# A hybrid SSD / RWKV-7 / mLSTM diffusion step on one core: the three output norms moved

## What is computed

```python
def _group_norm(y, g, n_groups, center, eps=1e-5):
    yf = y.reshape(y.shape[:-1] + (n_groups, y.shape[-1] // n_groups))
    if center:
        yf = yf - jnp.mean(yf, axis=-1, keepdims=True)
    yf = yf * lax.rsqrt(jnp.mean(yf * yf, axis=-1, keepdims=True) + eps)
    return yf.reshape(y.shape) * g
# SSD, 512 features, 2 groups of 256
y = (y_f + y_b + d_skip[:, None] * xs).reshape(b, t, D_SSD) * jax.nn.silu(z)
y_ssd = _group_norm(y, norm_g, SSD_GROUPS, center=False)
# RWKV-7, 256 features, 4 heads of 64 (o_f, o_b hold the bonus of r, k, r_k and v)
y_rwkv = _group_norm((o_f + o_b).reshape(b, t, D_RWKV), norm_g, RWKV_HEADS, center=True) * gate
# mLSTM, 256 features, 4 heads of 64
y_ml = _group_norm((h_f + h_b).reshape(b, t, D_MLSTM), norm_g, MLSTM_HEADS, center=True) * jax.nn.sigmoid(o)
y = jnp.concatenate([y_ssd, y_rwkv, y_ml], axis=-1) @ p['w_out']
```

## Time and profile before

| | us |
|---|---|
| median of 3 runs (lowest, highest) | 2300.25 (2297.17, 2303.04) |
| the profiled execution | 2307.51 |
| its span, mean granted clock 0.962 | 2305.8 |
| TensorE busy, products | 2129.9 (92%) |
| TensorE busy, weight loads | 1974.0 (86%) |
| VectorE busy | 836.0 (36%) |
| ScalarE busy | 774.3 (34%) |
| GpSimd busy | 735.9 (32%) |
| moved by DMA | 166.67 MB, 72 GB/s on the mean |

### The profile page before, as it was taken

One profiled execution on the slowest core, in us unless ns is written; L12 is line 12 of the kernel. 1 busy time (PEld: TensorE's weight loads), 2 busy tenths in 40 slices (PEclk: granted clock), 3 DMA queues, 4 the chain that ended last, 5 costly groups with the idle time before them and its releaser, 6 DMA issues.

```text
span 2305.8 us, 46139 instructions
## 1 busy us (share of the span) xinstructions
PE 2129.9 (92%) x20590; PEld 1974.0 (86%) x20590; DVE 836.0 (36%) x1385; ACT 774.3 (34%) x1368; POOL 735.9 (32%) x539
## 2 busy tenths in 40 slices
PE   4999999888789999999979989988888899999999
PEld 4999766778589999999979987667867899999998
DVE  4755265554641111011148443555455311110112
ACT  3535553323333222121144364433332422222212
POOL 4333161324123333333313322522242233333331
PEclk7999998999899999999989999899998899999999
DMA  7454201000012222234335431010001122222222
GB/s 250 147 156 128 63 8 37 6 2 3 19 55 65 80 76 74 74 110 142 104 87 174 148 114 30 1 38 5 3 2 46 50 79 74 74 74 74 73 76 71
DMA packets 260497, 166.67 MB, mean 72 GB/s; under 512 B 29938, under 2 KB 234228, under 8 KB 260300
## 3 DMA queue, kind: packets, MB, share of 16 engines
q1 hardware_dynamic: 259846, 163.59, 23.9%
q10 hardware_dynamic: 454, 0.14, 0.0%
HBM read 159.59 MB, written 4.12 MB: 71 GB/s over the span
## 4 chain that ended last, share of the span: by engine, by line
PE 84%; DVE 7%; ACT 5%; issue 2%; POOL 1%; DMA 0%; another core or an unknown queue 0%; SPq 0%; DVEq 0%; ACTq 0%
PE PS L928 21%; PE PS L929 20%; PE PS L930 20%; PE PS L1317 5%; PE PS L892 2%; PE PS L1462 1%; PE PS L1146 1%; PE PS L1383 1%; PE PS L1335 1%; PE PS L1183 1%; PE PS L989 1%; DVE U L2330 1%; PE PS L1197 1%; POOL ring_r L810 1%; PE PS L1150 1%
## 5 line engine op out<-in xcount | busy, mean ns | idle before, releaser
L928 PE MATMUL PS<-rwp_r,whi_r 128*128 128x320 f32 x2880 | 904.5, 314 | 40.4 <-POOL ring_r L810 16.5
L930 PE MATMUL PS<-rwp_r,ring_r 128*128 128x320 f32 x2880 | 896.6, 311 | 0.0
L810 POOL TENSOR_TENSOR ring_r<-ring,whi_r 128x1024 fp32r<-128x1024 f32 (+1 forms) x204 | 498.5, 2445 | 1139.7 <-ACT whi_r L1647 1139.7
L929 PE MATMUL PS<-arena_r,whi_r 128*128 128x320 f32 x2240 | 697.4, 311 | 0.0
L928 PEld LDWEIGHTS PS<-rwp_r,whi_r 128*128 128x128 f32 x2880 | 547.0, 190 | 56.0 <-issue 28.6
L930 PEld LDWEIGHTS PS<-rwp_r,ring_r 128*128 128x128 f32 x2880 | 546.9, 190 | 0.0
L929 PEld LDWEIGHTS PS<-arena_r,whi_r 128*128 128x128 f32 x2240 | 425.4, 190 | 0.0
L1647 ACT ACTIVATE whi_r<-ring 128x1024 fp32r<-128x1024 f32 (+1 forms) x204 | 211.4, 1039 | 542.1 <-PE PS L930 542.0
L929 PE MATMUL PS<-U_r,whi_r 128*128 128x320 f32 x960 | 298.2, 311 | 0.0
L2542 DVE TENSOR_TENSOR U<-arena,PS 128x640 f32<-128x640 f32 x44 | 36.2, 822 | 549.7 <-PE PS L930 549.7
L929 PEld LDWEIGHTS PS<-U_r,whi_r 128*128 128x128 f32 x960 | 181.8, 189 | 0.0
(11 more groups left out here) (383 smaller groups left out, 2667.7 us busy)
## 6 DMA issues: line engine op xcount, KB each, us to landing
ring<-in_ffn_w SPq DMA_DIRECT2D x120, 512.0 KB, 3.8
rwp<-in_ada_w SPq DMA_DIRECT2D x64, 512.0 KB, 4.8
ring<-in_w_in SPq DMA_DIRECT2D x50, 512.0 KB, 4.4
U<-in_ada_w SPq DMA_DIRECT2D x16, 512.0 KB, 9.7
ring<-in_w_out SPq DMA_DIRECT2D x16, 512.0 KB, 4.6
arena<-in_ada_w SPq DMA_DIRECT2D x16, 512.0 KB, 4.7
ring<-in_ffn_w SPq DMA_DIRECT2D x16, 384.0 KB, 3.3
out<-arena SPq DMA_DIRECT2D x5, 512.0 KB, 2.6
```

What stands on the lines that cost most here:

```text
L810: g.tensor_tensor(rings_r[:, slot_of[n], 0:size(n), :], slot(n)[:, 0:size(n), :], whis[:, q_ % 2, 0:size(n), :].bitcast(F32), ALU.subtract ...
L928: mm(out, w[0][:, k, :], hi[:, cols], start=start, stop=False)
L929: mm(out, w[0][:, k, :], lo[:, cols], start=False, stop=False)
L930: return mm(out, w[1][:, k, :], hi[:, cols], start=False, stop=stop)
```

## The change

SSD and mLSTM take their norms in two parts. In the scan, the sum of squares: for SSD, GpSimd multiplies each chunk by its gate (`gate(c)`), ScalarE squares it (`y_squares`), TensorE sums over features with a column of ones, so that a chunk's sums come with tokens on partitions (`y_sums`), VectorE copies them (`y_variance`). For mLSTM, `normalise` adds the two directions, centres, squares and sums with tokens on partitions (five VectorE instructions more), and `mlstm_back` is two transpositions in place of four products with the identity. The 30 columns `YN` of sums (2 groups and 4 heads, 5 chunks) get their square root on ScalarE at the end of RWKV's step 0 and their reciprocal on VectorE in step 1. `norm_rows`, in SyncE's queue ahead of w_out's block 2, writes them to DRAM with tokens as the last axis and reads them back broadcast over partitions, into `RBS` (SSD, in `whi`) and `ring_rows` (mLSTM, in the ring slot of block 2), and then waits until both are used. VectorE scales SSD's four tiles at the end of step 2, scales and gates mLSTM's two at the end of step 3. Their splits: `y_high` of three tiles at the end of step 3 and of three in step 4, `y_low` of three in step 4 and of three behind it.

The norm block keeps RWKV's own norm (centring, variance, one square root and one reciprocal of 64 partitions, scaling and gate), placed between w_out's rows: rows of tiles 0 to 2, centring, row 3, variance, rows 4 and 5, then the spread, then RWKV's two tiles. `YSEQ` is this order of the K tiles. A dummy square root stands ahead of it on ScalarE. The idle products are fewer: `warm` 6 to 2 and 8 to 4.

```diff
...
+yn_d = [nc.dram_tensor("yn%d" % l, (6, NC * P), F32, kind="Internal").ap() for l in range(DEPTH)]
...
+YSQ = [ar(9472 + 512 * i, 512) for i in range(2)]
+YS, YMEAN = ar(10496, 256), ar(4904, 4)
+RBS = whif[:, 0:2 * T].rearrange("p (g t) -> p g t", g=2)
...
+YSEQ = [0, 1, 2, 3, 6, 7, 4, 5]
+def ring_rows(lay):
+  at_ = KT * P * slot_of[SPLIT[lay * Q_LAYER + Q_WOUT + 2]]
+  return ring[:, at_:at_ + 2 * T].rearrange("p (f t) -> p f t", f=2)
...
+  def norm_rows():
+    sp.wait_ge(s["yn_rec"], at["yn_rec"] + 1)
+    load(yn_d[lay].rearrange("r (c t) -> t (r c)", c=NC), YN[:, :], s["yn_out"])
+    sp.wait_ge(s["yn_out"], at["yn_out"] + 16)
+    load(RBS, yn_d[lay][0:2].unsqueeze(0).broadcast_to((P, 2, T)), s["yn_in"])
+    for q in range(2):
+      load(ring_rows(lay)[64 * q:64 * q + 64],
+        yn_d[lay][2 + q:6:2].unsqueeze(0).broadcast_to((64, 2, T)), s["yn_in"])
+    sp.wait_ge(s["y_done"], at["y_done"] + 6)
   def rwkv_out():
...
+    if blk == (lay, "w_out", 2):
+      norm_rows()
...
   def gates():
-    pool.wait_ge(s["yt_read"], at["yt_read"] + NC)
-    pool.wait_ge(s["ys_read"], at["ys_read"] + NC)
-    g.tensor_tensor(U[:, XS:XS + 4, :], U[:, XS:XS + 4, :], U[:, Z:Z + 4, :], ALU.mult).then_inc(
-      s["gated"], 1)
-    pool.wait_ge(s["gated"], at["gated"] + 1)
-    pool.wait_ge(s["rw_ready"], at["rw_ready"] + 1)
...
+  def gate(c):
+    pool.wait_ge(s["ys_read"], at["ys_read"] + c + 1)
+    g.tensor_tensor(U[:, XS:XS + 4, ck(c)], U[:, XS:XS + 4, ck(c)], U[:, Z:Z + 4, ck(c)],
+            ALU.mult).then_inc(s["gated"], 1)
   def skip(c):
...
+      gate(c - 2)
+    for c in range(NC - 2, NC):
+      gate(c)
   def chunk_keys(k):
...
+  def y_sums(c):
+    pe.wait_ge(s["ysq_ready"], at["ysq_ready"] + c + 1)
+    for q in range(4):
+      n = 384 + 2 * c + q // 2
+      ins = mm(PS[:, 0, n:n + 1], YSQ[c % 2][:, q * P:(q + 1) * P], ones[:, 0:1],
+          start=q % 2 == 0, stop=q % 2 == 1)
+    ins.then_inc(s["ysq_mm"], 1)
   def y_mlstm(c):
...
-      for d in range(2):
-        ins = mm(PS[:, 6, f * P:(f + 1) * P], YM[:, d, f * P:(f + 1) * P], ident[:, :],
-            start=d == 0, stop=d == 1)
+      ins = tr(PS[:, 6, f * P:(f + 1) * P], YM[:, 0, f * P:(f + 1) * P], ident[:, :])
...
+      if c > 1:
+        y_sums(c - 2)
...
-  warm(6, 2)
+  y_sums(NC - 3)
+  warm(2, 2)
...
+  for c in range(NC - 2, NC):
+    y_sums(c)
   def cpos(k, d):
...
+  pe.wait_ge(s["ysq_read"], at["ysq_read"] + NC)
...
-        warm(8, 7)
+        warm(4, 7)
...
-  for n, t_ in enumerate((Z, Z + 1, MV, MV + 1)):
-    g_job(2 * n, [(BO[:, :], U[:, t_, :])]).then_inc(s["g_mm"], 1)
-  pe.wait_ge(s["g_read"], at["g_read"] + 4)
...
-    g_job(2 * ((2 + i) % 4), [(SPREAD[rows, :], gtmp[rows, 3, :])]).then_inc(s["g_mm"], 1)
   def residual_mm(b, w, k, hi, lo, start, stop):
...
-  pe.wait_ge(s["y_done"], at["y_done"] + 6)
+  def out_rows(seq):
+    for n in seq:
+      k = YSEQ[n]
+      pe.wait_ge(s["y_lo"], at["y_lo"] + n + 1)
+      for m in range(2):
+        ins = residual_mm(4 + 2 * m, w01[m], k, rp_r[:, k, :], U_r[:, YTILES[k], :], n == 0,
+                 n == KT - 1)
+        if n == KT - 1:
+          ins.then_inc(s["wo_mm"], 1)
+  for f in range(2):
+    g_job(2 * f, [(BO[:, :], U[:, Z + f, :])]).then_inc(s["g_mm"], 1)
...
-  for k, t_ in enumerate(YTILES):
-    pe.wait_ge(s["y_lo"], at["y_lo"] + k + 1)
-    for m in range(2):
-      ins = residual_mm(4 + 2 * m, w01[m], k, rp_r[:, k, :], U_r[:, t_, :], k == 0, k == KT - 1)
-      if k == KT - 1:
-        ins.then_inc(s["wo_mm"], 1)
+  out_rows(range(3))
+  pe.wait_ge(s["g_src"], at["g_src"] + 1)
+  for f in range(2):
+    g_job(2 * f, [(BO[:, :], U[:, BT_ + f, :])]).then_inc(s["g_mm"], 1)
+  out_rows(range(3, 4))
+  for f in range(2):
+    pe.wait_ge(s["g_read"], at["g_read"] + 4)
+    pe.wait_ge(s["g_sq"], at["g_sq"] + f + 1)
+    ins = g_job(0, [(BO[:, 48:80], gtmp[:, f, :])], slice(32 * f, 32 * f + 32))
+  ins.then_inc(s["g_mm"], 1)
+  out_rows(range(4, 6))
+  pe.wait_ge(s["g_rec"], at["g_rec"] + 1)
+  for f in range(2):
+    rows = slice(32 * f, 32 * f + 32)
+    g_job(2 * f, [(SPREAD[rows, :], gtmp[rows, 3, :])]).then_inc(s["g_mm"], 1)
+  out_rows(range(6, 8))
...
+  def y_squares(c):
+    act.wait_ge(s["gated"], at["gated"] + c + 1)
+    if c == 0:
+      act.wait_ge(s["stored"], at["stored"] + 7 * 16)
+    if c > 1:
+      act.wait_ge(s["ysq_mm"], at["ysq_mm"] + c - 1)
+    A(YSQ[c % 2].rearrange("p (f t) -> p f t", f=4), U[:, XS:XS + 4, ck(c)], ACT.Square).then_inc(
+      s["ysq_ready"], 1)
...
+      if i == 4 and c > 1:
+        y_squares(c - 2)
...
+  for c in range(NC - 2, NC):
+    y_squares(c)
+  def y_high(seq):
+    act.wait_ge(s["rw_feat"], at["rw_feat"] + 2 * NC)
+    act.wait_ge(s["rs_dve"], at["rs_dve"] + 2 * NC)
+    for n in seq:
+      act.wait_ge(s["y_done"], at["y_done"] + n + 1)
+      A(rp_r[:, YSEQ[n], :], U[:, YTILES[YSEQ[n]], :], ACT.Copy).then_inc(s["y_hi"], 1)
   def decays(k):
...
+    else:
+      y_high(range(3, 6))
...
+      act.wait_ge(s["ysq_read"], at["ysq_read"] + NC)
+      A(YN[:, 0:2 * NC], YN[:, 0:2 * NC], ACT.Sqrt, bias=eps[:, 2:3], scale=1.0 / 256)
+      A(YN[:, 2 * NC:], YN[:, 2 * NC:], ACT.Sqrt, bias=eps[:, 2:3], scale=1.0 / 64).then_inc(
+        s["yn_std"], 1)
+    if k == NC - 2:
+      y_high(range(3))
...
-  act.wait_ge(s["gated"], at["gated"] + 1)
-  act.wait_ge(s["yr_read"], at["yr_read"] + 2 * NC)
-  for q in range(4):
...
-    A(SQUARES[n], U[:, t_, :], ACT.Square).then_inc(s["g_sq"], 1)
+  A(NSD[:, :], NRC[:, :], ACT.Sqrt)
+  for f in range(2):
+    act.wait_ge(s["g_read"], at["g_read"] + 3 + f)
+    A(gtmp[:, f, :], U[:, BT_ + f, :], ACT.Square).then_inc(s["g_sq"], 1)
...
-  A(gtmp[0:64, 2, :].rearrange("p (a t) -> p a t", a=2), PS[0:64, 6:8, 0:HALF], ACT.Sqrt,
-   bias=eps[0:64, 2:3], scale=1.0 / 256).then_inc(s["g_std"], 1)
-  act.wait_ge(s["g_mm"], at["g_mm"] + 8)
-  A(gtmp[:, 3, :].rearrange("p (a t) -> p a t", a=2), PS[:, 4:6, 0:HALF], ACT.Sqrt,
-   bias=eps[:, 2:3], scale=1.0 / 64).then_inc(s["g_std"], 1)
-  for k, t_ in enumerate(YTILES):
-    act.wait_ge(s["y_done"], at["y_done"] + k + 1)
-    A(rp_r[:, k, :], U[:, t_, :], ACT.Copy).then_inc(s["y_hi"], 1)
+  A(gtmp[0:64, 3, :].rearrange("p (a t) -> p a t", a=2), PS[0:64, 0:2, 0:HALF], ACT.Sqrt,
+   bias=eps[0:64, 2:3], scale=1.0 / 64).then_inc(s["g_std"], 1)
+  y_high(range(6, 8))
...
-              (P, 2, 4, 64)), ALU.mult).then_inc(s["ym_ready"], 1)
+              (P, 2, 4, 64)), ALU.mult).then_inc(s["dve_step"], 1)
+    dve.wait_ge(s["dve_step"], step())
+    v.tensor_tensor(YS, YM[:, 0], YM[:, 1], ALU.add).then_inc(s["dve_step"], 1)
+    dve.wait_ge(s["dve_step"], step())
+    v.tensor_reduce(YMEAN, heads(YS, 4), AX.X, ALU.add).then_inc(s["dve_step"], 1)
+    dve.wait_ge(s["dve_step"], step())
+    v.scalar_tensor_tensor(out=heads(YM[:, 0], 4), in0=wide(YMEAN, 64), scalar=-1.0 / 64,
+               in1=heads(YS, 4), op0=ALU.mult, op1=ALU.add).then_inc(s["ym_ready"], 1)
+    dve.wait_ge(s["ym_ready"], at["ym_ready"] + c + 1)
+    v.tensor_tensor(YM[:, 1], YM[:, 0], YM[:, 0], ALU.mult).then_inc(s["dve_step"], 1)
+    dve.wait_ge(s["dve_step"], step())
+    v.tensor_reduce(YN[:, 2 * NC + c::NC], heads(YM[:, 1], 4), AX.X, ALU.add).then_inc(
+      s["dve_step"], 1)
+    dve.wait_ge(s["dve_step"], step())
+  def y_variance(c):
+    dve.wait_ge(s["ysq_mm"], at["ysq_mm"] + c + 1)
+    v.tensor_copy(YN[:, c:2 * NC:NC], PS[:, 0, 384 + 2 * c:386 + 2 * c]).then_inc(s["ysq_read"], 1)
   def prep_scan(k):
...
+    if c > 2:
+      y_variance(c - 3)
...
+  dve.wait_ge(s["ysq_mm"], at["ysq_mm"] + NC)
+  for c in range(NC - 3, NC):
+    y_variance(c)
   def chunk_start(k):
...
+  def y_scale(t_, nm, f, rows):
+    return v.scalar_tensor_tensor(out=U[:, t_, :], in0=U[:, t_, :], scalar=col(lay, nm, f),
+                   in1=rows, op0=ALU.mult, op1=ALU.mult)
+  def y_low(n):
+    k = YSEQ[n]
+    dve.wait_ge(s["y_hi"], at["y_hi"] + n + 1)
+    v.tensor_tensor(U_r[:, YTILES[k], :], U[:, YTILES[k], :], rp_r[:, k, :].bitcast(F32),
+            ALU.subtract).then_inc(s["y_lo"], 1)
...
+    else:
+      for n in range(3):
+        y_low(n)
+    if k == 1:
+      dve.wait_ge(s["yn_std"], at["yn_std"] + 1)
+      v.reciprocal(YN[:, :], YN[:, :]).then_inc(s["yn_rec"], 1)
...
+    if k == 2:
+      dve.wait_ge(s["yn_in"], at["yn_in"] + 16 * 3)
+      for f in range(4):
+        y_scale(XS + f, "ssd_norm_g", f, RBS[:, f // 2, :]).then_inc(s["y_done"], 1)
+    if k == 3:
+      for f in range(2):
+        ins = y_scale(MV + f, "mlstm_norm_g", f, ring_rows(lay)[:, f])
+      ins.then_inc(s["dve_step"], 1)
+      dve.wait_ge(s["dve_step"], step())
+      for f in range(2):
+        v.tensor_tensor(U[:, MV + f, :], U[:, MV + f, :], U[:, MO + f, :],
+                ALU.mult).then_inc(s["y_done"], 1)
+  for n in range(3, 6):
+    y_low(n)
   def pair(ap):
...
-  for n in range(2):
-    centre(MV + n, 4 + 2 * n, 3 + n)
...
-    centre(BT_ + n, 2 * n, 6 + n)
```

(16 more changed lines are left out.)

64 lines of the change are left out of this document (7 added, 57 removed).

## The result

The changed kernel takes 2354.73 us (median of 4 runs, 2342.99 to 2363.03), the kernel before 2298.71 us beside it: 2.5% slower, ratio 1.0247, 95% interval 1.0205 to 1.0289. The forecast was 2297, with a range up to 2315. The profiled execution of the changed kernel took 2357.4 us, the one of before 2307.51.

What follows compares the result with a forecast made beforehand. TensorE's chain (84%) bounds the kernel, its long hole per layer being the norm block. Per layer -19.7 (tail) + 7.4 (scan) + 9.1 (RWKV) + 1.8 (clock) = -1.4; twice -2.8 from 2300.25 gives 2297 us, range 2280 to 2315.

Steps and rivals of the forecast that it cites:

- SP's queue: SyncE's queue in RWKV: row write and read back estimated at 20 us against 58 available, so cost 0.
- the rows come late: Rival, end of step 2: 4-byte pieces take 100 us, VectorE and the recurrence stand; +50 per layer, 2400; chance 0.02.
- The scan: Scan: mLSTM's five VectorE passes delay the next decay products; together +7.4 us per layer (4.5 to 9.5).
- My steps: Scan terms: chunks 0 to 1 +2.3, 1 to 2 +1.5, 2 to 3 0, 3 to 4 +1.5, end +1.05 and +1.1.
- RWKV's steps: RWKV: step 1 +0.35, step 2's end +2.0, step 3's end +2.05, step 4 +4.7; together +9.1 us per layer.
- The +4.7 for the low halves of step 4: RWKV step 4: three y_low on VectorE held by GpSimd's port use, making the two adds behind late; +4.7 us.
- the sign that I had named: Step 4: y_low longer than 0.82 us beside GpSimd's scalings; running at 0.82 would mean the forecast is wrong, faster.
- the faster rival: Rival, step 4: y_low is not held by GpSimd's scalings; -7.0 us per layer, 2286; chance 0.34.
- the lower end of my bound: RWKV step 4: three y_low running bare, with the queue behind them, cost at least +0.4 us.
- The tail: Norm block behind RWKV's last add: 29.0 us in place of 48.8, at the full clock; 19.7 us less per layer.
- The clock rival: Rival: new TensorE holes bring 1.2 GHz in scan (4.4 us), two step ends and tail; +9.5 per layer, 2319; chance 0.22.
- 1.8 us for one hole: RWKV step 4: a TensorE hole of 4.6 us lowers the clock; 1.8 us counted per layer, other holes left uncounted.

Runs made afterwards that it cites:

- e1_rows: The changed kernel with the sums written to DRAM as 128 pieces of 120 bytes in place of 3840 of 4 bytes; 2327.48 us, ratio 1.0103.
- b2_write: The kernel before plus one DMA per layer, 30 idle columns written in 3840 pieces of 4 bytes in RWKV's step 1; 2326.63 us, ratio 1.0117.
- e2_no_mlstm: The changed kernel without mLSTM's five VectorE passes per chunk in the scan, directions added by four products as before; 2323.41 us, ratio 1.0102.
- e3_no_ssd: The changed kernel without SSD's squares, sums and their copies in the scan, a constant standing in; 2345.22 us, ratio 1.0169.
- e4_fill: The changed kernel with eight more idle products of 512 columns per chunk (1 to 4) on TensorE; 2330.95 us, ratio 1.0127.
- e9_all: The changed kernel with sums written in 512-byte pieces, scan passes, scalings and low halves moved, tail reordered, idle products added; 2281.21 us, ratio 0.9922.
- e10_nofill: As e9_all without its idle products (none in the scan, 2 and 4 behind it); 2267.41 us, ratio 0.9853 to the kernel before.

## Why the prediction was wrong

**SP's queue: the step that failed.** I costed the row write at 0, "unless a piece costs over four times that". The sentence asks only who waits for the rows, and in that it was right: the read back was in the rows' place by 495.5 and was needed at 542.6. It doesn't ask what the write does to an engine that doesn't wait for it. The price of a piece was not too low: 11.7 ns against the 34 that I took. But the queue went on only 17 us after the issue, and TensorE's semaphore came up to 6.8 us late meanwhile. The write cost 14.2 and 8.8 us (e1_rows, b2_write), nearly half of the loss. My rival "the rows come late" had the right culprit with the wrong victim, and only 0.02.

The Trainium skill, Runtime: NRT & Kernel Launch, section Instruction fetch mechanics, says that each engine's instructions are refilled in blocks of 16 KiB by a DMA queue of its own, and that this is mostly hidden. The trace agrees with the size (the packets of the instruction queue have 0.21 MB for 13). On the second it doesn't decide: one such packet took 5.4 us in this stretch, where TensorE stood, but in e2_no_mlstm's layer 0 TensorE stood too, with packets of 1.2 us alone.

The write explains nearly half. With it mended e1_rows takes 2327.5 us, still above 2315, and two more terms had failed, in the scan and in the clock.

**The scan.** The forecast was +7.4 with the end of the scan in step 0; it became +19.0 and +19.5. The passes' own part can be read from chunks at or near the full clock: 11.7, 15.2, 15.1, 15.0 and 14.4 us in b2_write's layer 0, against 14.6 (chunk 0), 17.1 (chunk 2) and 17.3 (chunk 4) in the changed kernel and 17.0 and 16.6 (chunks 1 and 3) in e3_no_ssd's layer 1. That is +2.9, +1.8, +2.0, +1.6 and +2.9, in all 11.2; at most, since chunks 2 and 4 of the changed kernel had 2.0 and 3.7 us at the low clock. My steps had +2.3, +1.5, 0, +1.5 and +1.05, and 1.1 more in step 0. The five passes are there as costed, between chunks 3 and 4 of the changed kernel:

```profile
391.22 0.42 DVE L2372 TENSOR_TENSOR arena<-arena 128x256 f32<-128x256 f32 x1
391.68 0.42 DVE L2374 TENSOR_REDUCE arena<-arena 128x4 f32<-128x256 f32 x1
392.13 0.42 DVE L2376 SCALAR_TENSOR_TENSOR arena<-arena 128x256 f32<-128x256 f32 x1
392.59 0.43 DVE L2379 TENSOR_TENSOR arena<-arena 128x256 f32<-128x256 f32 x1
393.05 0.42 DVE L2381 TENSOR_REDUCE YN<-arena 128x4 f32<-128x256 f32 x1
```

2.25 us, each 0.42 and its handover. The mis-sized terms are the last chunk and chunk 2, which I put at 0 because VectorE waited for TensorE there; that was so only at the low clock (in e3_no_ssd's layer 1, at the full clock, TensorE waits 1.79 us for VectorE behind chunk 2). The other 6.6 us of the scan's 17.8 (layer 0) go with the clock: 28.1 us more at 1.2 GHz, and e4_fill gives 11.8 us back with 32.3 fewer. It was my rival, with its place named, but I had one more slow chunk at 4.4 us; the slow time came to chunk 1 (25.3 and 21.7 us of it, 27.3 us at a stretch in layer 0) and chunk 3 (11.6 and 11.4).

Step 0 grew by 1.2 and 2.8 us. The fewer idle products ahead of it are not the reason: e9_all, with as many as before, has 40.7 and 42.3 us there, e10_nofill, with the few, 41.3 and 40.8.

**RWKV's steps.** +7.8 and +9.3 in steps 2 to 4, against 10.55: near, but by luck, since errors cancel. The two groups of scalings cost what was said (3.27 us on VectorE at the end of step 2, 2.0 on the chain). The +4.7 for the low halves of step 4 was wrong: GpSimd was held, not VectorE. Timeline of the changed kernel, step 4, for the earlier trace rows:

```profile
597.62 4.85 POOL L708 TENSOR_SCALAR U<-U,PC 128x640 f32<-128x640 f32 x2
...
598.51 2.29 DVE L2460 TENSOR_TENSOR U_r<-U,rwp_r 128x640 fp32r<-128x640 f32 x3
...
600.72 0.75 DVE L2492 TENSOR_TENSOR arena<-arena,PS 128x256 f32<-128x256 f32 x2
```

Three low halves take 2.29 us, each 0.82, bare; GpSimd's two scalings take 4.85 in place of 3.75. TensorE starts its next group as soon after the one ahead of it as in the kernel before (1.50 us in both; 561.59 in the earlier trace rows). So the sign that I had named (low halves longer than 0.82 each) did not appear. It is the faster rival's mechanism, and the lower end of my bound, 0.4, was the better value. In its place stands the clock: the hole that the scalings make at the end of step 3 is followed by 6.8 us at 0.50. Behind the scalings of step 2 it is alike: step 3 grew by 4.0 and 5.7 us, of which I had 2.0, with 10.2 and 12.3 us at the low clock in place of 3.4 and 1.4.

The rule of the Trainium skill that I weighed (SBUF — State Buffer, section Who interferes with whom) holds that a VectorE instruction with two SBUF inputs contends with a GpSimd instruction that reads SBUF, a one-input scaling too. The trace agrees in part: of GpSimd's two scalings the second takes 2.98 us in place of 1.88, while the low halves beside both keep their 0.82. Who loses is the point that decides, and here it was GpSimd.

**The tail.** -15.2 and -14.9 for -19.7. Every step of the order came as written, the port's included: the three low halves beside GpSimd's split take 6.19 us, the split 5.23. The term that failed is "at the full clock": 1.6 us on the first rows, 2.4 on the last; and 2.5 and 1.4 us more behind it, where I had nothing. The clock rival had this tail at +2.9.

**Clock, over all.** I gave 1.8 us for one hole and kept the rest as risk, 0.22. Over the whole execution the time at 1.2 GHz rose by 113 us (174.1 to 286.7). Some of that goes with the stalls of step 1, where it costs little. But holes of 2 to 4 us at the handovers of the scan, at the ends of steps 2 and 3 and in the tail were what the change put into TensorE's work, and the sum should have priced each of them.

**Where the gain is.** The idea was sound: the tail's long hole can be emptied. e10_nofill does the same computation in the same places with the write in 512-byte pieces, VectorE's passes behind what TensorE waits for, and the chain of the tail started first: 2267.4 us, ratio 0.9853.

**Still open.** Why the scan of before has 14 to 16 us at the low clock in one profile and 0.3 to 3.7 in b2_write's with the same code is not settled; neither is SSD's share in the scan. How the write of 4-byte pieces stops TensorE is open too: a slow fetch packet stands beside eight of ten stalls, mostly ending too late to have ended them, and which engine a fetch packet belonged to isn't in the trace.

## What to carry to other kernels

Before moving work from a hole into a busy loop, ask of each pass not how long it is but what is queued behind it: here the same passes cost 11 us per layer ahead of the decay products and 3 to 4 behind them, and nothing between RWKV's later adds. A DMA that nobody waits for is not free: count its pieces, and where they are of 4 bytes transpose on chip first. A wait that a profile puts down to nobody can be one of its own engines: look at when the semaphore rose. Idle products keep the clock only where a hole is; elsewhere they cost time.

## What the runs showed of the hardware

A write of 15 KB in 3840 pieces of 4 bytes took 17 us from issue until the read back could start and lengthened the step in which it lay by 8 to 14 us; the same bytes in 128 pieces of 120 landed in 1.4, in 30 pieces of 512 in 1.3 us. The pieces took 11.7 ns each on the mean in the changed kernel; TensorE's semaphore rose 4 to 7 us late in all ten steps with such a write. Fetch packets of 1.1 us took up to 6.6 us beside it in eight of them, and none did in two. When VectorE's two-input passes met GpSimd's work, it was GpSimd's scaling that got longer in step 4 (3.75 to 4.85 us), but VectorE's passes that got longer beside the weight split (6.19 us for three, against 2.29). And TensorE at 1.2 GHz with hardly an idle microsecond (26.09 of 27.3) can cost a scan more than the wait that came before it.
